# Sticks, gated unit, group norms and the first block of the output product written as one program

## The reference, cut to what matters

```
o_b = b_gate * (conv_w[0]*z[t-2] + conv_w[1]*z[t-1] + conv_w[2]*z[t]),  z = c_gate * h      # mixer B
u, v = split(gelu(cols));  o_c = u * (tril(sgu_w) @ layer_norm(v) + sgu_b)                  # mixer C
z = q @ k.T / 8;  log_1m = where(mask, log_sigmoid(z) - z, 0)                               # mixer D, 8 heads
tail = cumsum(log_1m, reverse=True) - log_1m;  a = where(mask, exp(log_sigmoid(z) + tail), 0);  o_d = a @ v
mixed = rms_norm([o_a, o_b, o_c, o_d], group_gain)        # per group of 512
x = x + mixed @ w_out
```

## Time and profile before

| | us |
|---|---|
| median of 3 runs (3115.95 to 3120.32) | 3116.26 |
| the profiled execution | 3121.72 |
| its span, first to last instruction | 3120.0 |
| TensorE busy | 3026.1 |
| VectorE busy | 1957.6 |
| ScalarE busy | 1456.8 |

### The profile page before, as it was taken

One profiled execution on the slowest core, in us unless ns is written; L12 is line 12 of the kernel. 1 busy time (PEld: TensorE's weight loads), 2 busy tenths in 40 slices (PEclk: granted clock), 3 DMA queues, 4 the chain that ended last, 5 costly groups with the idle time before them and its releaser, 6 DMA issues.

```text
span 3120.0 us, 46831 instructions
## 1 busy us (share of the span) xinstructions
PE 3026.1 (97%) x19141; PEld 2765.1 (89%) x19141; DVE 1957.6 (63%) x2731; ACT 1456.8 (47%) x2147; POOL 171.6 (6%) x314
## 2 busy tenths in 40 slices
PE   8998599999998999999999999999999999999999
PEld 7987587888887887978789999999999999999999
DVE  4654445444444445454557988888777777777766
ACT  4353534444343444354444467447744444444453
POOL 2000100000000000140000000000010000000000
PEclk9998799999999999999999999999999999999999
DMA  7553065565664554544567779768998878888764
GB/s 245 172 160 119 27 199 167 188 188 188 191 189 156 191 197 147 168 145 162 177 217 245 243 260 340 231 225 301 344 370 311 296 281 315 308 299 295 248 216 135
DMA packets 222012, 690.97 MB, mean 221 GB/s; under 512 B 14250, under 2 KB 95178, under 8 KB 170625
## 3 DMA queue, kind: packets, MB, share of 16 engines
q1 hardware_dynamic: 204640, 598.71, 57.4%
q0 software_dynamic: 12608, 71.73, 5.9%
q10 hardware_dynamic: 4576, 17.89, 1.6%
HBM read 652.61 MB, written 33.57 MB: 220 GB/s over the span
## 4 chain that ended last, share of the span: by engine, by line
PE 50%; DVE 1%; ACT 0%; ACTq 0%; issue 0%; DVEq 0%
PE banks L2267 16%; PE banks L2268 8%; PE banks L2341 7%; PE banks L2340 7%; PE banks L2342 7%; PE banks L2314 2%; PE banks L2361 1%; PE banks L2363 1%; PE banks L2362 1%; DVE weights_lo L195 0%; DVE peer_scratch L2687 0%; PE banks L2286 0%; DVE peer_features L369 0%; PE banks L2330 0%; PE banks L2303 0%; PE banks L2339 0%
## 5 line engine op out<-in xcount | busy, mean ns | idle before, releaser
L195 DVE TENSOR_TENSOR weights_lo<-weights,weights_hi 128x1024 fp32r<-128x1024 f32 (+4 forms) x1080 | 1227.8, 1178 | 810.9 <-ACT weights_hi L188 809.6
L188 ACT ACTIVATE weights_hi<-weights 128x1024 fp32r<-128x1024 f32 (+4 forms) x1080 | 1047.0, 1018 | 1427.2 <-PE banks L444 655.0
L2267 PE MATMUL banks<-peer_features,weights_hi 128*128 128x448 f32 (+1 forms) x2304 | 737.2, 376 | 1.7 <-DVE weights_lo L195 1.6
L442 PE MATMUL banks<-weights_hi,features_hi 128*128 128x512 f32 (+3 forms) x1600 | 606.1, 379 | 24.2 <-DVE weights_lo L195 24.1
L2268 PE MATMUL banks<-peer_features,weights_lo 128*128 128x224 f32 (+1 forms) x2304 | 615.0, 267 | 0.0
L444 PE MATMUL banks<-weights_hi,features_lo 128*128 128x512 f32 (+3 forms) x1600 | 601.2, 376 | 0.0
L443 PE MATMUL banks<-weights_lo,features_hi 128*128 128x512 f32 (+3 forms) x1600 | 601.1, 376 | 0.0
L2341 PE MATMUL banks<-applied_lo,weights_hi 128*128 128x224 f32 x2048 | 562.7, 275 | 0.0
L2342 PE MATMUL banks<-applied_hi,weights_lo 128*128 128x224 f32 x2048 | 562.6, 275 | 0.0
L2340 PE MATMUL banks<-applied_hi,weights_hi 128*128 128x224 f32 x2048 | 562.5, 275 | 0.0
L2267 PEld LDWEIGHTS banks<-peer_features,weights_hi 128*128 128x128 f32 x2304 | 431.9, 187 | 41.6 <-DVE weights_lo L195 1.8
(11 more groups left out here) (404 smaller groups left out, 2503.0 us busy)
## 6 DMA issues: line engine op xcount, KB each, us to landing
weights<-in_expert_u SPq DMA_DIRECT2D x128, 1024.0 KB, 5.2
weights<-in_expert_v SPq DMA_DIRECT2D x128, 1024.0 KB, 5.8
weights<-in_w_ffn_gate SPq DMA_DIRECT2D x44, 1024.0 KB, 5.2
weights<-in_w_ffn_up SPq DMA_DIRECT2D x44, 1024.0 KB, 5.2
weights<-in_w_ffn_down SPq DMA_DIRECT2D x44, 1024.0 KB, 4.9
weights<-in_w_in SPq DMA_DIRECT2D x48, 900.0 KB, 4.8
weights<-in_w_out SPq DMA_DIRECT2D x32, 1024.0 KB, 5.2
weights<-in_w_in SPq DMA_DIRECT2D x24, 704.0 KB, 4.4
```

The costliest lines, as they stand in the source:

```text
L188: act.activation(hi[:, k, n], raw[:, k, n], ACT.Copy).then_inc(self.hi_ready, 1 + skip)
L195: last = dve.tensor_tensor(lo[:, k, n], raw[:, k, n], hi[:, k, n].bitcast(F32), ALU.subtract)
L442: pe.matmul(out, xh, wh, start=first, stop=False)
L2267: pe.matmul(self.bank(n % 3, 2 * (T - lo)), wh[:, k, :], F[:, k, :, lo:T], start=(k == 0), stop=False)
```

## The change

The one-token shifted copy doesn't wait for job 5; it goes to the tile `normed`, and the load of `sgu_w`, which went there early on, goes to `nsa_k` after job 5. The convolution's passes 1 to 6 move to steps 44 to 47. The transposes of `sgu_w` and of mixer D's queries and keys move into steps 43 and 46 of the input product, with their copies out of PSUM behind them (ScalarE at 45 and 47, VectorE at 47), and POOL masks `sgu_w` at that product's end. A mask of 0 and -1e30 (`stick_mask`) is made by POOL at the start, and VectorE adds it where it scales the scores, in place of POOL's masks.

`sticks_sgu` is no longer a program of its own. It returns functions that `linear` runs: `*_first` ahead of the output product's first step, and `tensor`, `scalar`, `vector` between its first four steps. Step n needs the features of mixer n alone (0 is A), so A and B are normed and turned first (`turn`, `feature_hi`, `feature_lo`: the transposes, the high and the low part of two feature rows), C after step 1, D after step 2. The programs `turn_stage` and `norm_groups` are gone from here. The diff, cut:

```diff
                         for half in range(2):
                             if turned is None:
                                 self.turn_split(src, hT, gains, None, *sides, part=half)
-                            split(eng, stream, 0, 0, half)
+                            if turned is None or "gpsimd" not in turned:
+                                split(eng, stream, 0, 0, half)
                         if turned is not None:
                             turned["scalar" if name == "act" else "vector"](eng)
...
+        def tensor_first(pe):
...
+                last.then_inc(scored, 1)
+            pe.wait_ge(gdone, 2)
+            for j in range(4):
+                if j >= 2:
+                    pe.wait_ge(rd.sem, rd.at(j - 1))
+                turn(pe, j)
+            tails(pe, 0)
+            pe.wait_ge(rd.sem, rd.at(4))
+
+        def tensor(pe, n):
+            if n == 0:
+                tails(pe, 1)
+                pe.wait_ge(normed, 1)
+                pe.wait_ge(weighed, 1)
+                for t in range(NT):
...
+            if n == 1:
...
+                pe.wait_ge(exped, 2)
+                pe.wait_ge(weighed, 2)
...
+                pe.wait_ge(gdone, 4)
+                for j in (4, 5):
+                    turn(pe, j)
+                pe.wait_ge(rd.sem, rd.at(6))
+            if n == 2:
+                pe.wait_ge(gdone, 6)
+                for j in (6, 7):
+                    turn(pe, j)
+                pe.wait_ge(rd.sem, rd.at(8))
...
+        def scalar_first(act):
+            ch = self.act_chain.on(act)
+            ch(act.activation(junk[:, 0, :], group(0, 0), ACT.Square, accum_out=stat(0, 0)))
+            ch(act.activation(junk[:, 0, :], group(1, 0), ACT.Square, accum_out=stat(1, 0)))
+            act.sem_inc(gsq, 1)
+            for t in range(NT):
+                last = act.activation(v[:, t, :], C[:, t, 512:1024], ACT.Gelu_apprx_tanh, accum_out=self.stat[:, 4 + t:5 + t])
+            last.then_inc(summed, 1)
+            act.activation(C[:, :, 0:512], C[:, :, 0:512], ACT.Gelu_apprx_tanh)
+            act.wait_ge(grs, 1)
+            act.activation(group(0, 0), group(0, 0), ACT.Copy, scale=rstd(0, 0))
+            act.activation(group(1, 0), group(1, 0), ACT.Copy, scale=rstd(1, 0)).then_inc(gdone, 1)
+            for g in range(2):
+                act.wait_ge(negd, g + 1)
+                act.activation(of(L, g), of(L, g), ACT.Exp).then_inc(expd, 1)
+                act.wait_ge(expd, g + 1)
+                act.activation(of(L, g), of(L, g), ACT.Ln, bias=1.0).then_inc(logd, 1)
+                for j in (2 * g, 2 * g + 1):
+                    feature_hi(act, j)
+            act.wait_ge(centred, 1)
+            for t in range(NT):
+                last = act.activation(junk[:, t, :], v[:, t, :], ACT.Square, accum_out=self.stat[:, t:t + 1])
+            last.then_inc(squared, 1)
+            for half in range(2):
+                ring.split_hi(act, stream, 0, 0, half)
+            for g in range(2):
+                act.wait_ge(weighed, g + 1)
+                act.activation(of(Z, g), of(Z, g), ACT.Exp).then_inc(exped, 1)
+            act.wait_ge(gread, 1)
+            act.activation(junk[:, 0, :], group(2, 0), ACT.Square, accum_out=stat(2, 0)).then_inc(gsq, 1)
+            act.wait_ge(grs, 2)
+            scale_act(act, 2, 0, group(2, 0))
+
+        def scalar(act, n):
+            if n == 2:
+                for j in (4, 5):
+                    feature_hi(act, j)
+                for t in range(NT):
+                    act.wait_ge(mixed, t + 1)
+                    last = act.activation(junk[:, t, :], self.bank(mbank(t)), ACT.Square, accum_out=stat(3, t))
+                last.then_inc(gsq, 1)
+                act.wait_ge(grs, 3)
+                scale_act(act, 3, 0, self.bank(mbank(0)))
+            if n == 3:
+                for j in (6, 7):
+                    feature_hi(act, j)
...
+        def vector_first(dve):
...
+            ch(square_dve(dve, 0))
+            square_dve(dve, 1).then_inc(gsq, 1)
+            for g in range(2):
+                dve.wait_ge(scored, g + 1)
+                for (z, n), (p, _) in zip(tiles(Z, g), tiles(self.psum[:, 2 * BANK:2 * BANK + 2 * GW], g)):
+                    last = dve.scalar_tensor_tensor(out=z.rearrange("p (h t) -> p h t", h=4), in0=p.rearrange("p (h t) -> p h t", h=4),
+                                                    scalar=HD ** -0.5, in1=self.later[:, 0:n].unsqueeze(1).to_broadcast([P, 4, n]),
+                                                    op0=ALU.mult, op1=ALU.add)
+                ch(last)
+                dve.scalar_tensor_tensor(out=of(L, g), in0=of(Z, g), scalar=-1.0, in1=of(Z, g), op0=ALU.mult, op1=ALU.min)\
+                    .then_inc(negd, 1)
+                if g == 0:
+                    dve.wait_ge(grs, 1)
+                    scale_dve(dve, 0, group(0, 1))
+                    scale_dve(dve, 1, group(1, 1)).then_inc(gdone, 1)
+            dve.wait_ge(summed, 1)
+            ch(dve.tensor_scalar(self.stat[:, 8:10], self.stat[:, 4:6], 1.0 / BANK, None, ALU.mult))
+            for t in range(NT):
+                last = dve.tensor_scalar(v[:, t, :], v[:, t, :], self.stat[:, 8 + t:9 + t], None, ALU.subtract)
+            last.then_inc(centred, 1)
+            softplus(0)
+            for j in (0, 1):
+                feature_lo(dve, j)
+            softplus(1)
+            for j in (2, 3):
+                feature_lo(dve, j)
+            exponents(0)
+            dve.wait_ge(rs, 1)
+            for t in range(NT):
+                last = dve.tensor_scalar(v[:, t, :], v[:, t, :], self.rstd[:, t:t + 1], None, ALU.mult)
+            last.then_inc(normed, 1)
+            for half in range(2):
+                ring.split_lo(dve, stream, 0, 0, half)
+            exponents(1)
+            dve.wait_ge(gmixed, 1)
+            bias = self.gT[:, G_SGUB:G_SGUB + NH].unsqueeze(2).to_broadcast([P, NH, HD])
+            for t in range(NT):
+                last = dve.tensor_tensor(v[:, t, :].rearrange("p (h d) -> p h d", h=NH),
+                                         self.bank(2 + t).rearrange("p (h d) -> p h d", h=NH), bias, ALU.add)
+            ch(last)
+            dve.tensor_tensor(C[:, :, 0:512], v[:, :, :], C[:, :, 0:512], ALU.mult).then_inc(gread, 1)
+            dve.wait_ge(gread, 1)
+            square_dve(dve, 2).then_inc(gsq, 1)
+            dve.wait_ge(grs, 2)
+            scale_dve(dve, 2, group(2, 1)).then_inc(gdone, 1)
...
+            if n == 43:
+                pe.wait_ge(sgu_loaded, 16)
+                pe.wait_ge(shifted, len(JOBS))
+                for b in range(2):
+                    transposes(4 + b, [self.sgu_w[:, 4 * b + h, :] for h in range(4)])
+            if n == 46:
+                for t in range(NT):
+                    pe.wait_ge(self.bank_free[t].sem, left(D_OFF + 1024))
+                pe.wait_ge(ra.sem, ra.at(startup + 6))
+                pe.wait_ge(out_read, len(JOBS))
+                for i in range(4):
+                    at = D_OFF + i * 2 * P
+                    transposes(4 + i, [PR[:, t, at + kk * P:at + (kk + 1) * P] for kk in range(2) for t in range(NT)])
...
-            if n in CONV:
-                conv_step(CONV.index(n))
-
-        CONV = [32, 40, 42, 44, 45, 46, 47]
+            if n == 47:
+                for i in range(2):
+                    dve.wait_ge(tr.sem, tr.at(startup + 13 + i))
+                    dve.tensor_copy(stick_k[:, 2 * i:2 * i + 2, :].rearrange("p k t -> p (k t)"), self.bank(6 + i)).then_inc(rd.sem, 1)
+            for k in [k for k, at_step in enumerate(CONV) if at_step == n]:
+                conv_step(k)
+
+        CONV = [32, 44, 45, 45, 46, 46, 47]
...
             for s in (2, 1):
-                if s == 1:
-                    pool.wait_ge(scored, 6)
                 ch(pool.memset(z[s - 1][0:s, 0, :], 0.0))
                 pool.dma_start(z[s - 1][s:P], x1[0:P - s]).then_inc(moved, 16)
                 pool.dma_start(z[s - 1][0:s, 1, :], x1[P - s:P, 0, :]).then_inc(moved, 16)
+            pool.wait_ge(scored, 6)
+            pool.dma_start(self.sgu_w, a["sgu_w"][0].rearrange("h p q -> p h q")).then_inc(sgu_loaded, 16)
             pool.wait_ge(moved, 16 * 5)
-            pool.wait_ge(sgu_loaded, 16)
+            pool.wait_ge(ra.sem, ra.at(startup + 6))
+            ch(pool.affine_select(out=wT, in_=wT, pattern=[[0, NH], [1, P]], compare_op=ALU.is_ge, fill=0.0, base=0,
+                                  channel_multiplier=-1))
...
-            self.sticks_sgu(PR)
             hT = self.features(ctx, KD)
-            offs = (0, B_OFF, C_OFF, D_OFF)
-            self.norm_groups(lambda t, g: PR[:, t, offs[g]:offs[g] + BANK], 4, BANK)
-            self.linear(s_out, s_up, hT, chunk(self.XN), self.gains_of(G_GROUP, KD), BANK, self.add_out, ("dve", "dve"))
+            turned, under = self.sticks_sgu(ctx, PR, s_out, hT)
```

(2 more changed lines are left out.)

336 lines of the change are left out of this document (139 added, 197 removed).

## The result

The changed kernel takes 3091.89 us (median of 4 runs, 3087.92 to 3093.86), the one before 3116.11 (4 runs, 3115.85 to 3120.32): a ratio of 0.9916, 95% interval 0.99 to 0.9931, so 24.2 us less. 3087 was predicted, in a range of 3079 to 3100. The profiled execution took 3093.86 (3121.72 before), with a span of 3092.2 and a mean granted clock of 0.991.

The account below looks back on a forecast made before the run. TensorE is busy almost throughout, so only its standstills can give: minus 14.5 us in the input product and minus 15.2 up to and within the output product's first steps, minus 29.7 together. From 3116.3 that predicted 3087, range 3079 to 3100.

Parts of the forecast that it names:

- slow copy lands: Input product: the one-token copy, started near 203 us instead of 233.65, has its last piece land near 241 us.
- end of the input product: TensorE's input product ends at 302.8 us instead of 317.3, minus 14.5, as the wait for the copy goes.
- from there to the first step: From the input product's end to the output product's first matmul: 29.8 us instead of 66.9, minus 37.1.
- step 1, loss by its slow start: Output product's first step, after a 5 us TensorE pause: charged the whole slow start measured behind the stall, 2.9 us.
- two pauses: Within the output product's first four steps: TensorE waits twice for its last transposes to pass ScalarE and VectorE, 2.3 us each.
- less than one engine was busy: During TensorE's stall the DMA share was 0.05, less than one of sixteen engines; a spread-out half-megabyte copy would look different.
- the 40 us of cover: Input product: copy landing near 241 us, first convolution pass needing it about 281, so the wait is gone.
- Weights late: Rival, chance 0.08: the slow copy delays weight fills in the input product's steps 34 to 40; 6 us lost, 3093.
- The rival of a round more: Rival, chance 0.16: one wrong wait on ScalarE's and VectorE's chain before the first step adds 5.6 to 7.3 us; 3094.
- 1.38 us for each switch of table: ScalarE drain per table switch: five ahead of the first split start it 6.9 us later, 3094; no separate chance given.
- Given back: Output product's first four steps: tails, gate, outputs, transposes, pauses and a slow start inside them cost plus 21.9 us.
- rival of a lasting low clock: Rival, chance 0.04: pauses keep TensorE's clock low; through four steps 3117, no change, through six steps 3127.

Follow-up runs that it names:

- e1: Changed kernel with the convolution's part undone: one-token copy waits for job 5 again, passes at steps 40, 42, 44 to 47; 3107.57 us, ratio 0.9958.
- e3: Kernel before with only the convolution's passes moved to the changed kernel's later steps, copies starting as before; 3102.06 us, ratio 0.994.
- e2: Changed kernel with only the one-token copy held back until job 5, passes staying at steps 44 to 47; 3089.95 us, ratio 0.9903.
- e11: Changed kernel with the convolution's passes back at steps 40, 42, 44 to 47, the one-token copy still early; 3092.07 us, ratio 0.9913.
- e4: Kernel before with the 127-partition one-token copy issued as two transfers, 112 and 15 partitions; 3100.66 us, ratio 0.9945.
- e12: e9 with POOL's mask of sgu_w waiting for ScalarE's copy at step 47 instead of those of step 45; 3079.54 us, ratio 0.9874.
- e5: Changed kernel run again unaltered, as the base for later runs; 3091.29 us, ratio 0.9914 to the kernel before.
- e10: Changed kernel with ScalarE taking both exponentials, then both logarithms, so two table loads fewer; 3087.78 us, ratio 0.9894.
- e6: Changed kernel with TensorE's pauses ahead of output-product steps 1, 3 and 4 filled by idle transposes (40, 16, 16); 3085.93 us, ratio 0.9896.
- e8: Changed kernel with mixer C's transposes ahead of the sticks' outputs instead of behind them; 3086.85 us, ratio 0.9896.
- e7: Changed kernel with the first half of the first step's weights split earlier on ScalarE and VectorE; 3086.32 us, ratio 0.9898.
- e9: Changed kernel with the edits of e6 (24 transposes ahead of step 1, 16 ahead of step 4), e7 and e8 together; 3081.83 us, ratio 0.9869.

## Why the prediction held, and where its terms were off

Both stalls went as predicted, and each of the two places paid alone (11.7 us for the new program in e1, 17.2 for the copy's part in e3). The times below are those of the profiled execution:

| term | predicted | measured |
|---|---|---|
| slow copy lands | 241 | 241.7 |
| end of the input product | 302.8 | 305.44 |
| from there to the first step | 29.8 | 28.35 |
| step 1, loss by its slow start | 2.9 | 2.57 |
| tails of the second half | 3.7 | 3.47 |
| gate | 3.5 | 3.49 |
| outputs | 5.3 | 5.30 |
| four remaining pairs' transposes | 1.9 | 2.07 |
| two pauses | 4.6 | 4.38 |
| slow starts of steps 3 and 4 | 0 | 3.4 |
| end of the fourth step | 376.3 | 380.4 |

**The input product.** That the wait goes is shown by the traces and by e1. It was argued with two reasons that weren't separable, an early landing and a later reader; e2, e3 and e11 show that either is enough. The prediction's aside that less than one engine was busy pointed at the shape, and e4 shows that this is the root. The end came 2.6 us late. Of this 0.73 is the idle at 288.44, behind the add that POOL's mask of sgu_w stretches, as e12 shows. The prediction gave that mask no price at all: its sum of VectorE's work around step 45, which it put at nothing with 1.5 us to spare, was right in its own durations (the passes took 1.22 for 1.2 predicted) and didn't ask what POOL does beside them. Another 1.5 is the low clock from 267.3 to 270.8: from the instruction at 265.35 us to that at 280.61 pass 15.3 us, where e5 has 13.7 for the same work. It isn't a cost of the change: the second execution doesn't have it. The last 0.4 has no single place. Pass 1 began at 285.0 us, not at 281, which the 40 us of cover took without harm.

**Weights late** (the rival at 0.08) did not happen: fills beside the copy landed after 15.3 and 16.8 us, and in e2 even 21.6 brought no wait of ScalarE.

**The chain to the first step** was walked to 28.7 + 1.1 and measured at 28.35, 27.2 behind the first score. ScalarE's part, from the first score to the squares of v, came out as 21.6 us for 23.3. The rival of a round more (0.16) falls, and so does that of 1.38 us for each switch of table: the Trainium skill (ScalarE: Activation LUTs, What ACT_TABLE_LOAD costs) adds that drain, while in the rows of ScalarE above each load of 1.28 us is joined to what stands beside it within 0.02 us. That the alternation has two loads more than it needs costs nothing on the chain, as e10 shows: they buy an early softplus.

**Given back.** Five of the terms are within 0.25 us. The step that failed is the clock at steps 3 and 4: the pauses were costed at their length alone (4.6), and the slow start was charged to the first step, as the one behind 5 us of pause. Here each pause of 2.19 us is followed by a slow start too, of 1.73 and 1.68 us (7.18 and 7.13 for a step that takes 5.45). That the pauses are the cause is shown by the counts under e6: 12 of 15 such pauses have a slow step behind them, and none of ten that were filled or removed. The term is therefore not a fixed price: by these counts an estimate is 12/15 of 3.4, 2.7 us.

**The sum.** 2.6 later at the product's end, 1.45 less to the first step, 2.9 more given back: the fourth step ends 4.1 us later than predicted, 25.6 earlier than before (406.03 in that trace). The rest of the program took 2711.8 us here and 2714.0 before. e5 has 2714.4 with the same kernel, so that these 2.2 us are spread between executions and no part of the change; they hid half of the miss, which was luck. The median is 4.9 us above the prediction: the forecast took from the execution's 3092 the 5.4 us by which the profiled execution of before lay above its median, and this one lies 2.0 above. The rival of a lasting low clock (0.04) falls: from the first step on it ends within some 6 us of matmuls each time. Ahead of that step the clock does stand at 0.50, from 308.3 to 325.4 us, through most of the scores, the turnings and the first tails. At the scores it costs nothing, as ScalarE sets the pace: in e2 all the scores ran at full clock, and the first step came 28.36 us after the product's end, no earlier.

**Left open.** It stays open why 3 of the 15 pauses of 2.19 us, all in the same two places, were not followed by the low clock, and why some executions have the low stretch at 267 us, with TensorE busy throughout: the changed kernel's first, e3, e4, e6, e8, e11 and e12 have it, e2, e5, e7, e9 and e10 don't. It follows neither the copy nor the steps. Also open is whether the two parts add up: 11.7 and 17.2 make 28.9, where the whole gave 24.2 and 26.4, but e1's interval alone is 10 us wide.

## What to carry to other kernels

Read the low DMA share beside a long landing as a transfer on few engines, and change its shape (112 + 15 partitions for 127) before moving what waits for it. Where TensorE must pause ahead of a product, expect a slow start behind most pauses, those of 2 us too (12 of 15 here), and remove the pause by reordering or fill it with idle transposes. Before costing a small POOL instruction at nothing, look at what VectorE does beside it.

## What the runs showed of the hardware

- A copy from SBUF to SBUF of 127 partitions, 508 KB, holds what is queued behind it for 33.9 to 35.6 us; as 112 and 15 partitions it lands in 3.6 and 3.2 us, and one of 126 partitions, 504 KB, in 3.8.
- In the changed kernel a pause of TensorE of 2.19 us was followed by 3.6 us at a clock of 0.53 to 0.54, one of 5.7 us by 5.4 us at 0.51. Over eight traces 12 of 15 pauses of 2.19 us were followed by the low clock and 3 were not; behind 1.84 us in the kernel before, 2.62 in e7, 1.32 in e6 and 0.44 in e9 it stayed at 1.00. The length of the last pause alone doesn't decide it.
- A clock of 0.51 to 0.59 over 3.5 us came with TensorE busy throughout, in 7 of the 12 traces that work through 267 us, and of two traces of the same kernel in one.
- POOL's affine_select (1.10 us, 128 x 1024) stretches a VectorE add of two SBUF operands from 0.69 to 1.55 us, and leaves a copy out of PSUM as it is.
